# The low parts of the front stages' weight tiles move to VectorE, and 56 of 96 modulation steps move behind the expert tables' gates

## What is computed

```python
def conv_ffn(h, w_up, conv_w, conv_b, w_down):
    u = einsum('bsd,df->bsf', h, w_up)                       # 256 x 5632
    up = pad(u, 2 rows in front)
    u = conv_b + sum(conv_w[j] * up[:, j:j + S] for j in range(3))
    gate, val = u[..., :2816], u[..., 2816:]
    return einsum('bsf,fd->bsd', silu(gate) * val, w_down)

# second block, layer i: six modulation vectors from c
sh1, sc1, g1, sh2, sc2, g2 = split(silu(c) @ ada_w[i] + ada_b[i], 6)   # ada_w[i]: 1024 x 6144
hx = xs * (1 + sc1) + sh1                    # i = 0: also the context rows, with silu(c_ctx)
xs = layer_norm(alpha * xs + g1 * mixer(hx), ln_g[i, 0], ln_b[i, 0])
hx = xs * (1 + sc2) + sh2
f = peer(hx)      # routing, then gelu(hx @ U.T) at the chosen experts, weighted, @ V
xs = layer_norm(alpha * xs + g2 * f, ln_g[i, 1], ln_b[i, 1])
```

## Time and profile before

| | |
|---|---|
| median of 3 runs | 2619.42 us |
| the profiled execution | 2617.04 us, of which the span 2615.7 us |
| mean granted TensorE clock | 0.942 |
| TensorE matmuls busy | 91% of the span |
| VectorE, ScalarE, GpSimd busy | 72%, 42%, 24% |
| read from HBM | 436.88 MB, 168 GB/s over the span |

### The profile page before, as it was taken

The page is one execution under the profiler, slowest core; times in us unless marked ns, Lnnn a source line. Parts: engine busy times, 40 slices in busy tenths (PEclk is TensorE's granted clock), DMA queues, the critical chain, the costliest instruction groups (busy, mean ns, idle before and its releaser), DMA issues.

```text
span 2615.7 us, 38981 instructions
## 1 busy us (share of the span) xinstructions
PE 2380.1 (91%) x15710; PEld 2090.3 (80%) x15710; DVE 1895.9 (72%) x3144; ACT 1104.8 (42%) x1571; POOL 633.4 (24%) x252
## 2 busy tenths in 40 slices
PE   5778887788978999999999999889999999999997
PEld 4667777566746999999977788668999999777786
DVE  9766999777375488777788755674887777888555
ACT  3234433242354444444444444444444444444443
POOL 6513655655304344200000000153433000000000
PEclk8767988889988999999999999899999999999999
DMA  7536556743303555555555655534555455555653
GB/s 278 167 111 201 185 189 203 282 148 113 105 1 113 170 179 178 168 167 165 169 170 173 209 190 188 183 121 165 182 177 170 163 169 169 169 170 180 220 187 121
DMA packets 123202, 442.58 MB, mean 169 GB/s; under 512 B 13696, under 2 KB 16768, under 8 KB 122256
## 3 DMA queue, kind: packets, MB, share of 16 engines
q1 hardware_dynamic: 117288, 425.04, 49.0%
q10 hardware_dynamic: 5736, 15.06, 1.6%
HBM read 436.88 MB, written 3.16 MB: 168 GB/s over the span
## 4 chain that ended last, share of the span: by engine, by line
PE 73%; DVE 18%; issue 4%; ACT 3%; DMA 1%; POOL 1%; ACTq 0%; DVEq 0%; SPq 0%
PE ps L352 22%; PE ps L353 22%; PE ps L354 22%; DVE acc L1421 6%; PE ps L2239 2%; DVE cv L1672 1%; DVE hT L1402 1%; DVE hT L1400 1%; PE ps L380 1%; DVE xr L1903 1%; ACT spl L906 1%; DVE xr L1898 1%; DVE spl L2047 1%; POOL spl L2296 1%; PE ps L2188 1%
## 5 line engine op out<-in xcount | busy, mean ns | idle before, releaser
L2296 POOL TENSOR_TENSOR spl<-ring,spl 128x1024 fp32r<-128x1024 f32 (+1 forms) x239 | 624.8, 2626 | 1380.2 <-ACT spl L906 1379.8
L906 ACT ACTIVATE spl<-ring 128x1024 fp32r<-128x1024 f32 x703 | 735.4, 1051 | 528.3 <-PE ps L354 512.3
L2047 DVE TENSOR_TENSOR spl<-ring,spl 128x1024 fp32r<-128x1024 f32 x464 | 573.0, 1235 | 449.0 <-ACT spl L906 448.8
L352 PE MATMUL ps<-hT,spl 128*128 128x256 f32 x2656 | 774.3, 292 | 40.1 <-POOL spl L2296 30.2
L353 PE MATMUL ps<-hT,spl 128*128 128x256 f32 x2656 | 762.8, 287 | 0.0
L354 PE MATMUL ps<-hT,spl 128*128 128x256 f32 x2656 | 762.0, 287 | 0.0
L352 PEld LDWEIGHTS ps<-hT,spl 128*128 128x128 f32 x2656 | 520.7, 196 | 49.5 <-POOL spl L2296 34.5
L353 PEld LDWEIGHTS ps<-hT,spl 128*128 128x128 f32 x2656 | 521.9, 196 | 0.2 <-issue 0.2
L354 PEld LDWEIGHTS ps<-hT,spl 128*128 128x128 f32 x2656 | 520.9, 196 | 0.0
L352 PE MATMUL ps<-spl,Ws 128*128 128x512 f32 x1024 | 409.9, 400 | 0.2
L353 PE MATMUL ps<-spl,Ws 128*128 128x512 f32 x1024 | 404.4, 395 | 0.0
(11 more groups left out here) (368 smaller groups left out, 2594.2 us busy)
## 6 DMA issues: line engine op xcount, KB each, us to landing
ring<-in_peer_u SPq DMA_DIRECT2D x256, 512.0 KB, 3.5
ring<-in_peer_v SPq DMA_DIRECT2D x256, 512.0 KB, 3.5
aring<-in_ada_w SPq DMA_DIRECT2D x96, 512.0 KB, 4.3
ring<-in_w_up SPq DMA_DIRECT2D x44, 512.0 KB, 3.8
ring<-in_ab_in SPq DMA_DIRECT2D x32, 512.0 KB, 3.4
ring<-in_peer_wq SPq DMA_DIRECT2D x32, 512.0 KB, 4.3
ring<-in_w_down SPq DMA_DIRECT2D x22, 512.0 KB, 4.4
ring<-in_w_in SPq DMA_DIRECT2D x20, 512.0 KB, 4.7
```

Source lines behind the costliest of these rows:

```text
L352: q.matmul(o, l[0], r[0], start=start, stop=False)
L906: q.activation(P.spl[:, m % SPLITS, 0, 0:w], P.ring[:, m % SLOTS, 0:w], ACT.Copy).then_inc(*P.hi.mark(m))
L2047: q.tensor_tensor(P.spl[:, n % SPLITS, 1, 0:w], P.ring[:, n % SLOTS, 0:w], P.spl[:, n % SPLITS, 0, 0:w].bitcast(F32), ALU.subtract).then_i ...
L2296: q.tensor_tensor(P.spl[:, n % SPLITS, 1, 0:w], P.ring[:, n % SLOTS, 0:w], P.spl[:, n % SPLITS, 0, 0:w].bitcast(F32), ALU.subtract).then_i ...
```

## The change

- `lo_on_dve` is true for every tile before the "ab" stage: 97 low parts move from line 2296 (GpSimd) to line 2047 (VectorE), placed by hand in VectorE's loops. GpSimd has no low part to form before tile 97.
- `ada_plan` is a list of places: 8 steps in "in", 3 in "wo", 5 in "up", 24 in "dn", none in "ret" and "mla"; 48 steps among the last 62 V tiles of layer 0 (five of every six tiles have one), 8 among those of layer 1. The folds stand at ret 7, up 42, dn 9, dn 17, ab 6, six of them among layer 0's V tiles and one among layer 1's.
- The moved steps have their own ring, accumulators and bias rows, where the gate planes of the first V half lay, so their loads wait until those are read (`ws 63`). A memset of the bias rows on GpSimd goes before.
- In "up" VectorE and ScalarE treat block n - 1 while they split the tiles of block n.
- "dn" accumulates in banks 4, 5, 6, 2 instead of 0 to 3. A gate fold has two banks and waits for no copy between its two matmuls. The context mask loads move to slot 8 of "in". The layer-norm rows are fetched at V tile 100 instead of 63. The merge of norm gains into the modulation vectors is cut in three (`dve_folds`).

```diff
-    room = [("in", n, 1) for n in range(20)] + [("ret", h, 1) for h in range(8)] + [("mla", h, 1) for h in range(10)]
-    room += [("wo", n, 1) for n in range(8)] + [("up", n, (n + 1) % 2) for n in range(44)]
-    room += [("dn", n, 2) for n in range(22)]
...
+    places = [("in", n) for n in (4, 6, 10, 12, 13, 15, 16, 18)]
+    places += [("wo", n) for n in (2, 4, 6)] + [("up", 2 * f) for f in (2, 6, 10, 14, 18)]
+    places += [("dn", k) for k in range(22)] + [("dn", 8), ("dn", 16)]
+    places.sort(key=lambda s: (("in", "wo", "up", "dn").index(s[0]), s[1]))
+    places += [("v", 0, 66 + s + s // 5) for s in range(48)] + [("v", 1, 66 + 2 * s) for s in range(8)]
+    for s, slot in enumerate(places):
+        put("step", s, *slot)
+    folds = [("ret", 7), ("up", 42), ("dn", 9), ("dn", 17), ("ab", 6)]
+    folds += [("v", 0, places[8 * i + 7][2] + 3) for i in range(5, 11)] + [("v", 1, 84)]
...
 def lo_on_dve(n):
...
-    return False
+    return n < T_AB
...
 def dve_in(q, P):
...
         hilo(q, dve, P.hT, k, P.xTf[:, k, :], ("hT", k))
+        if k % 2:
+            dve_lo(q, P, k // 2)
...
     for n in range(20):
+        dve_lo(q, P, n + 2)
         dve_ada(q, P, ("in", n))
...
 def dve_up(q, P):
...
+    for n in range(23):
+        f = n - 1
+        dve_lo(q, P, T_UP + 2 * n + 2)
+        if f >= 0:
+            q.wait_ge(*act.at(("ev", f)))
...
+        if n < 22:
+            dve_lo(q, P, T_UP + 2 * n + 3)
+            for part in range(2):
+                dve_ada(q, P, ("up", 2 * n + part))
+        if f >= 0:
+            s = P.sg[:, f % 2, :]
+            q.wait_ge(*act.at(("silu", f)))
...
 def dve_down(q, P):
     pe, act, dve = P.stage("dn")
     for k in range(22):
+        dve_lo(q, P, T_DN + k + 2)
         dve_ada(q, P, ("dn", k))
...
     for j in range(66, 128):
         dve_lo(q, P, T + 144 + j)
         dve_ws(q, P, j, act, dve)
+        dve_ada(q, P, ("v", l, j))
...
     for j in range(64, 128):
         pe_v(q, P, l, j)
+        pe_fold(q, P, ("v", l, j))
...
+    after = {5: [("bias", 0), ("bias", 1)] + [("step", s) for s in range(ASLOTS)]}
+    for l, s0 in enumerate((40, 88)):
+        after[T_PEER[l] + 144 + 69] = [("bias", s0 // 8)] + [("bias", 6)] * (l == 0) + [
+            ("step", s) for s in range(s0, s0 + ASLOTS)]
```

More of the change, by code:

```diff
@@ L368, in pe_fold @@
             q.wait_ge(*fold_out(P, i - 1))
+        if slot[0] == "ab":
+            q.wait_ge(*P.stage("ab")[1].at(("turn", 7)))
         if ADA_TASK[i][1] in (2, 5):
+            if slot[0] == "dn":
+                q.wait_ge(*P.stage("up")[2].at(("conv", 21)))
             for n in range(2):
[L371 to L374, removed]
+                q.matmul(banks[n][:, :], P.ones[:, :], acc[:, ada_half(i), n * 512:(n + 1) * 512], start=True,
+                         stop=True).then_inc(*P.ada_pe.mark(("gate", i, n), ("fold", i)))
         else:
             for z in range(2 if ada_two(i) else 1):
[L377 to L382, removed]
+                for m in range(8):
+                    t = q.matmul(banks[0][:, 8 * z + m:8 * z + m + 1],
+                                 acc[:, z if ada_two(i) else ada_half(i), m * 128:(m + 1) * 128],
+                                 P.ones[:, 0:1], start=True, stop=True)
+                t.then_inc(*P.ada_pe.mark(("cols", i, z), ("fold", i)))
 def fold_out(P, i):
@@ L1206, in act_diff @@
     act_ln_rows(q, P, "abo", 0, 0)
-    q.wait_ge(*P.line("gate3_stored").at("row"))
+    q.wait_ge(*P.ada_pe.at(("fold", ADA_FRONT - 1)))
     for name, b0, dst in (("QT", 2, P.QT), ("KT", 6, P.KT[:, :, 256:512])):
@@ L1285, in act_peer @@
     tmp = P.ln[key][3][:, :].rearrange("p (a n) -> p a n", a=4)
-    q.wait_ge(*P.stage("ab")[2].at("folds"))
+    q.wait_ge(*before[2].at("folds"))
     act_turned(q, pe, act, P.ps, tmp, P.adc[:, l, 3, :], P.adc[:, l, 2, :])
@@ L1405, in dve_ada @@
 def dve_ada(q, P, slot):
-    for kind, i in ADA_PLAN[slot]:
+    for kind, i in ADA_PLAN.get(slot, []):
         if kind == "step":
             task, k = i // 8, i % 8
+            ring, acc, abr, row = P.ada(task)
             q.wait_ge(*P.ald[i % ASLOTS].at(i))
@@ L1731, in dve_ab @@
         bb = 0 if i % 2 == 0 else 4
+        for p in range(4):
+            dve_ada(q, P, ("ab", 4 * i + p))
+        if i == 4:
+            q.wait_ge(*P.line("gate0_stored").at("row"))
         if 2 <= c < 6:
@@ L2291, in pool_program @@
     for n in range(T_END):
+        for l in range(2):
+            if n == T_PEER[l] + 208:
+                q.wait_ge(*P.stage(f"peer{l}")[2].at(("ws", 63)))
+                q.memset(P.vbr[:, :, :], 0.0).then_inc(*c.mark(("vbr0", l)))
         if lo_on_dve(n):
@@ L2378, in sp_program @@
         sp_load(q, P, n)
[L2379 to L2383 removed]
+        for kind, i in ada.get(n, []):
+            (sp_ada if kind == "step" else sp_ada_bias)(q, P, i)
     o = P.out.rearrange("(t p) d -> p t d", p=128)
```

237 lines of the change are left out of this document (123 added, 114 removed).

## The result

The changed kernel takes **2482.93 us** (median of 4 runs, 2481.64 to 2485.61) against 2620.85 us (4 runs, 2614.26 to 2625.99) of the kernel before: ratio 0.9476, 95% interval 0.9453 to 0.9500. The forecast was 2483.0. The profiled execution took 2483.58 us, its span 2482.2, at a mean granted clock of 0.961 (0.942 before).

The account below looks back on a forecast made before the run. VectorE waiting for GpSimd inside its instructions bounds the front, TensorE the V tail. Savings of 161 us less 24.5 given back, 136.5, from 2617.0 make 2480.5; 2.4 added for the median: 2483 us, range 2454 to 2528.

Parts of the forecast that it names:

- the good ends: Lower end of the range, 2454 us: V tail giving back 13 us and "up" lasting 127 us.
- rival 3: Ring traffic or ScalarE, not GpSimd, stretches VectorE wherever tiles stream, so the kernel gets slower: 2890 us, chance 0.03.
- rival 4: The change doesn't do what it says and GpSimd still forms front tiles: 2619 us, chance 0.01.
- "In" (50, measured 51.1): Stage "in" falls from 125 to 75 us by the sum of VectorE's loop, saving 50.
- "dn" (46.5, 49.6): Stage "dn" falls from 116 to 69.5 us, saving 46.5; between 34, if loads fall behind, and 50.
- "Up" (52, measured 47.4): Stage "up" falls from 183 to 131 us, 22 blocks of 5.6 us led by TensorE, saving 52.
- I take 2.80 also for a tile of 24 matmuls of 256 columns: In "up", such a TensorE tile takes 2.80 us like a V tile, having the same number of columns.
- The 4 us for the five double steps: In "up", five blocks with a double step (2.4 us more VectorE work each) cost some 4 us in all.
- "Wo" (2, measured -0.3): Stage "wo", 37 us, saves 2: a fold goes (2.0), three double steps are covered by 22 us of matmuls.
- The V tails (24.5, measured 30.0): V tails give back 24.5 us: folds 15.5, waits behind four column folds 7.2, first step loads 2; bounds 13 and 80.
- a sign of being wrong: Wrong would be TensorE waiting on VectorE's low parts in most "up" or V-tail tiles, or VectorE waiting on step loads.
- Rival 1: The front's engines mesh less well, TensorE's clock drops and "dn" loads fall behind: 2515 us, chance 0.19.

Follow-up runs that it names:

- e1: The changed kernel with the front's 97 low parts back on GpSimd, steps left where the change put them: 2540.21 us.
- e5: The changed kernel without the lag of a block in "up", each block treated right behind its own pair of tiles: 2495.22 us.
- e8: e4 with the three double steps of "wo" moved into "up", eight there instead of five: 2471.95 us.
- e3: The changed kernel with VectorE's copy of a column fold three V tiles later, the fold itself left in place: 2466.33 us.
- e7: e4 with a step in every one of 48 V tiles of layer 0, not in five of six: 2466.08 us.
- e4: e3 with the first step of layer 0's V tail at tile 68 instead of 66: 2462.09 us.

## Why the prediction was right

Right in total, and by its own mechanism in every large term. That 2483 met 2482.93 is luck: the terms are off by up to 5.5 us each way (table above) and cancel to 2.9, and the 2.4 us added for the median of the kernel before cancels what is left, since the changed kernel's median lies 0.65 below its profiled execution. One bound doesn't follow either: the V tail and "up" at the good ends that the prediction names give 2483 - 11.5 - 4 = 2467.5, not 2454.

**What stretches VectorE.** The whole forecast rested on low parts of 1.14 and steps of 1.19 us from start to start with GpSimd silent. Measured in the front: 1213 ns for 97 low parts, 0.43 for a subtraction, 1.28 to 1.32 for a step. e1 shows that GpSimd alone is the cause, so rival 3 (2890) is out, and so is rival 4: GpSimd is busy for 2.79 us before "dn", and its first low parts are the mixer's.

**"In" (50, measured 51.1) and "dn" (46.5, 49.6).** VectorE is busy 62 of 73.8 us in "in". TensorE waits for its low parts 15.2 us in 5 times, of which 9.0 are the wait for the very first. The sum by VectorE's loop held in its end (the 14 low parts behind tile 5's were done at 71.3 us, forecast 71.5), though tile 5's own began at 27.4 us where 29.5 was assumed; VectorE stood for only 2.3 us between. But TensorE stood for only 2.2 us behind 28.7 us, so there both engines were nearly full. "Dn" came out better, since the loads are no limit. Windows of 10 us:

```profile
340.00:350.00 10.00, 10.00 (x45) 8.02 (x44) 9.24 (x9) 3.94 (x4) 0.00 (x0) 1.00 0.99 394
350.00:360.00 10.00, 10.00 (x41) 7.44 (x40) 7.58 (x8) 4.36 (x5) 0.00 (x0) 1.00 1.03 409
360.00:370.00 10.00, 10.00 (x44) 8.03 (x43) 9.45 (x9) 3.79 (x4) 0.00 (x0) 1.00 0.99 374
```

The DMA engines move 374 to 409 GB/s while they are full. The Trainium skill's figure of some 358 GB/s for HBM (page "DMA: Bandwidth & Descriptors", section "Where 436 GB/s comes from"), by which the sum would have been 2 us worse, doesn't bind here; the measurement decides.

**"Up" (52, measured 47.4): terms off both ways.** The step that failed is "I take 2.80 also for a tile of 24 matmuls of 256 columns". TensorE's block is 5.76 us, 2.88 per tile: twice as many matmuls for the same columns, each with its own weight load. That is 22 x 0.16 = 3.5 us. The 4 us for the five double steps were in turn too much: with the lag they cost nothing, without it e5 pays 8.0 us of waits for them. What the lag earns, 11 us of "up" by e5, the prediction costed at nothing and had in its block's sum. The rest is the first tile, which follows its activations' low parts and takes 5.0 us (189.99 to 195.00) instead of 2.88, and the last one, behind the double fold, which takes 5.3 us (319.8 to 325.0); the clock is 0.70 from 320 to 330 us. These two had no term; they make 4.5 us.

**"Wo" (2, measured -0.3).** The step "three double steps are covered by 22 us of matmuls" was wrong. TensorE waits only 0.3 us for a low part there, but the last two double steps (173.12 and 177.79 us) stand in VectorE's queue ahead of the residual additions (line 1687, at 181.31), and the norm and the transposes of "up" wait for those. Before these transposes TensorE stands for 6.4 us, where it stood for 4.2 before the change; without the steps, in e8, it stands for 4.5, and the stretch gets 2.4 us back.

**The V tails (24.5, measured 30.0).** TensorE waits 1.8 us behind each of three column folds, as forecast, and 3.5 behind the fourth, where GpSimd stretches the low part; besides, it waits 1.7 us for a first load (forecast 2). That first load is the one place where VectorE waited for a step's load for long (4.56 us), which the prediction had named as a sign of being wrong. Layer 0's folds were a little cheaper (10.8 us against 13). The missing term is the clock behind the waits at folds, 6 to 7 us; e3 takes both away at once. VectorE at 2.67 of 2.80 us and loads of 343 GB/s held, and e7 shows room beyond.

**Rival 1** (engines mesh worse) did not come: TensorE is busy 134.7 of 135.0 us in "up" and all of "dn".

## What to carry to other kernels

If VectorE's instructions end when GpSimd's end, taking GpSimd's work over can shorten VectorE's own busy time; read it off the same instruction where GpSimd is idle before moving anything. An engine that copies out what another has just computed should get that copy a few tiles later than it becomes ready, or everything queued behind the copy stops; here TensorE stood for it, and its clock fell behind the stand. Before loading more onto an engine that "has slack", divide its whole work in the stage, steps included, by the number of blocks and compare with the bound engine's.

## What the runs showed of the hardware

**A column fold of 1.84 us didn't lower TensorE's clock, a fold with a stand behind it did.** With the same 16 one-column matmul records over 1.84 us, the granted clock over 50 us was 0.93 where TensorE stood for 1.8 us behind two of them, and 1.00 where it went on at once (windows above). A stand of 1.72 us without a fold left it at 1.00 too. The double fold of 32 records in "up" (3.80 us) had no stand behind it, and the clock from 320 to 330 us was 0.70.

**The front differs from run to run by up to 5 us in the same code.** The first transposes of "mla" began at 115.8 us in the changed kernel, 113.4 in e3, 110.6 in e4, 112.7 in e7 and 115.9 in e8. Windows right behind "in", of the changed kernel and of e4:

```profile
80.00:90.00 10.00, 9.45 (x44) 7.89 (x44) 3.87 (x12) 5.84 (x15) 0.00 (x0) 0.83 0.12 49
90.00:100.00 10.00, 9.27 (x40) 7.88 (x40) 7.27 (x21) 2.44 (x3) 0.00 (x0) 0.69 0.34 102
```

```profile
80.00:90.00 10.00, 9.22 (x54) 7.72 (x54) 5.05 (x13) 7.96 (x17) 0.00 (x0) 1.00 0.00 0
90.00:100.00 10.00, 9.55 (x47) 8.10 (x47) 9.34 (x33) 0.00 (x0) 0.00 (x0) 0.77 0.33 107
```

TensorE is as busy in both (18.7 and 18.8 us), yet by these clocks it spends 9.6 of the 20 us at the lower level (1.2 GHz) in one and 4.6 in the other, and the records that it gets through are 84 and 101. Differences of 4 or 5 us between medians of such kernels are therefore not evidence by themselves; the V tails, which agree within 0.2 us between e4, e7 and e8, are.

**256-column matmuls.** They start every 0.120 us, 2.88 us for a tile of 24, where 12 of 512 columns at 0.233 take 2.80. In "up" the records show the weight loads busy all the time (133.33 of 135.00 us in the window above), in the V tail 80% of it; that they are what paces the shorter matmuls fits this and was not tried.
